# A hybrid decoder layer on one core: 24 instead of 16 tokens gathered, adds ahead of softmaxes, memory loads at other points

## The chip, the cores and the metric

The kernel runs on 1 core of one Trainium2 chip. The metric is the device time of one execution in microseconds (us).
## The reference

One inference step of a decoder layer, in float32, for 256 prompt tokens and 64 sample tokens (8 requests of 8 tokens) that share the weights:

```
x = x + merge(dilated_attention(h), window_attention(h))   # h = rmsnorm(x), one input projection
x = x + cross_attention(rmsnorm(x), memory keys, memory values)   # 4 heads of 128, 256 memory tokens
x = x + peer(rmsnorm(x))
y = rmsnorm(x)

def peer(xb):            # 128*128 experts of one neuron, 8 heads, the 16 best of each head
    q = (xb @ w_pq).reshape(T, 8, 256)
    s1, s2 = q[..., :128] @ sub_k1.T, q[..., 128:] @ sub_k2.T
    # top 16 of each half, top 16 of their 256 sums -> eidx (T, 8, 16), gate = softmax(best)
    act = gelu(einsum('td,thkd->thk', xb, expert_u[eidx]))
    return einsum('thk,thkd->td', gate * act, expert_v[eidx])
```

The model width is 2048; expert_u and expert_v have 16384 rows of 2048 float32 each, 128 MB apiece.

## The kernel before

The 320 tokens lie as two groups of columns: tile 0 (128 tokens, `FIRST_TILE`) and the rest (192 tokens, `THE_REST`: 128 of the prompt, called tile 1 below, and the 64 sample tokens). Up to about 460 us the input projection and the prompt attention run. From there to about 665 us a loop over the 8 requests (`for n in range(REQ)`, lines 1115 and 1715) does the sample attention; between its steps TensorE does output projection, cross-attention query and output tiles of tile 0 (`OUT_WITH`, line 98: which tiles stand ahead of the scores, with the scores, and with the turning of the probabilities). VectorE adds each output tile to the stream (`add_to_stream`, line 887) and does the softmax of the next request (`softmax_s`). A tile may start when the tile two before it has been added, as two PSUM banks take turns. Then, to about 1000 us, come the output projection, cross-attention and query projection of the rest, with tile 0's expert choice on VectorE between them.

SP loads all dense weights as chunks of 1 MB into a ring of four slots (`WR`); a chunk's load is issued when TensorE has used the chunk four before it. `mem_keys(g)` (2 MB) and `mem_values(g)` (four times 0.5 MB) load the memory of requests 4g to 4g+3 in that same list of SP, both g into the same buffers (`km`, `vm`).

The experts are done in two ways. For tile 0, each of the 128 (head, k) choices is one **row**: an indirect DMA by POOL brings one expert of each of the 128 tokens (1 MB, line 539 for expert_u, line 545 for expert_v), and VectorE does the dot product (`u_dot`, line 1240) or the weighted sum (`v_row`, line 1253). Sixteen tokens of tile 1 (`FEW`) are gathered too: their 8 heads stand on 8 groups of 16 partitions, so 16 more rows do for all of them. Rows in all: `ROWS` = 144 for u and 144 for v. Three buffers (`URING`) take the u rows, four (`VRING`) the v rows; a gather is issued when the row three (four) before it has been used. The other 176 tokens (`DENSE`) are multiplied with all experts: 128 chunks of expert_u, then 128 chunks of expert_v, each chunk 16 matmuls of 128x128 by 128x176. Every float32 matmul is two instructions on PE, so a chunk is 32. Their gates are built as maps: VectorE makes one-hots from the turned choices (line 1354), ScalarE weighs them (line 793), TensorE multiplies them (4 tokens, 8 instructions a map), VectorE applies them (line 1364). There are `MAPS` = 44 maps, spread over the u chunks from `MAP_LO` = 100 to 124.

The order around the change, by position: VectorE has done u rows 0 to 140 (`ROWS_BEFORE` = 141) and then copies the turned choices (lines 1343 to 1345) and signals `choices_kept`; TensorE turns the choices after u chunk 91 (`TURN` = 92) and waits for `choices_kept` at the first map, in chunk 100. ScalarE moves the choices of the 16 tokens to other partitions with 8 small DMAs after chunk 79 (`few_choices_in`); POOL waits for them ahead of row 128. From chunk 103 on (`DOTS_DONE` = 102) VectorE's slots between the maps, 1 or 2 rows a chunk, hold v rows. After v chunk 95 TensorE adds the sum of the 16 tokens (`h_few`) through `pick`.

## Time and profile before

| what | value |
|---|---|
| median of 3 runs | 2308.41 us (2307.99 to 2311.57) |
| the profiled execution's own time | 2311.11 us |
| its span in the trace | 2309.2 us |
| PE, PEld, DVE, ACT, POOL busy | 96%, 87%, 51%, 13%, 17% |
| granted PE clock over the span | 0.984 |
| moved by DMA | 843.21 MB, mean 365 GB/s |

Times inside the trace count from the start of the span. "Busy" of PE is modelled for pipelined matmuls, so a PE that is 100% busy may still start its matmuls at a slower pace; the number of instructions in a stretch tells the pace. What stands in square brackets behind a row of a timeline is the idle time ahead of it and what ended it.

### The profile page before, as it was taken

What the parts mean: (1) busy time and instruction counts of PE and PEld (TensorE: products, weight loads), DVE (VectorE), ACT (ScalarE), POOL (GpSimd) and SP (SyncE); (2) the same over time, 40 slices, a digit from 0 to 9 for tenths busy, and PEclk for the clock granted to TensorE, in tenths of its full rate; (3) what the DMA queues carried; (4) which work ended last, traced back from release to release, by engine and by line L of the source; (5) the groups of instructions that cost most, each with busy time, mean ns of one, the idle gap of its engine ahead of it and who ended that gap; (6) DMA issues with size and microseconds to landing.
All of it is one profiled execution on the core that took longest, in us unless ns stands there. A gap on an engine that the chain in (4) does not pass through costs nothing.

```text
span 2309.2 us, 35404 instructions
## 1 busy us (share of the span) xinstructions
PE 2207.9 (96%) x14282; PEld 2015.7 (87%) x14282; DVE 1179.1 (51%) x2095; ACT 301.2 (13%) x926; POOL 386.3 (17%) x414
## 2 busy tenths in 40 slices
PE   7999998789889879999999999999999999999998
PEld 5677776577589868999999999899999999999998
DVE  3200003833566647767777544599744444444422
ACT  2000001722221012011111110144200000000000
POOL 0100000022302011232212221133311111111100
PEclk9999999999999989999999999999999999999999
DMA  7999982289959898999999999999999999999974
GB/s 280 405 413 381 385 316 81 80 333 357 398 201 396 345 383 315 407 398 422 422 421 420 420 420 420 372 372 376 402 422 421 422 422 421 422 422 422 421 315 155
DMA packets 117787, 843.21 MB, mean 365 GB/s; under 512 B 14432, under 2 KB 16608, under 8 KB 30656
## 3 DMA queue, kind: packets, MB, share of 16 engines
q1 hardware_dynamic: 62752, 485.30, 52.4%
q0 software_dynamic: 54128, 354.58, 37.7%
q10 hardware_dynamic: 816, 2.11, 0.2%
q8 instruction: 58, 0.95, 0.2%
q14 instruction: 33, 0.27, 0.0%
HBM read 834.25 MB, written 74.78 MB: 394 GB/s over the span
## 4 chain that ended last, share of the span: by engine, by line
PE 64%; DMA 23%; DVE 8%; issue 2%; ACT 1%; POOL 1%; SPq 0%; DVEq 0%; POOLq 0%; ACTq 0%
PE low L1414 39%; PE big L1414 24%; DMA BIG<-expert_u,VB 20%; DVE BIG L1240 4%; DMA WR<-wall 1%; DMA BIG<-kaT 1%; ACT BIG L630 1%; DMA BIG<-expert_v,VB 1%; DMA BIG<-memT 0%; DMA BIG<-va 0%; DVE CST L968 0%; POOL BIG L525 0%; DVE BIG L846 0%; PE low L1538 0%; DVE HT L883 0%
## 5 line engine op out<-in xcount | busy, mean ns | idle before, releaser
L1414 PE MATMUL low<-HT,WR 128*128 128x176 f32 (+3 forms) x6336 | 1081.9, 333 | 8.4 <-DMA WR<-wall 7.0
L1414 PEld LDWEIGHTS low<-HT,WR 128*128 128x128 f32 x6336 | 984.2, 191 | 98.2 <-issue 9.7
L1414 PE MATMUL big<-BIG,WR 128*128 (+3 forms) x2888 | 450.7, 312 | 11.3 <-DVE XT L891 7.1
L1253 DVE SCALAR_TENSOR_TENSOR XT<-BIG,VB,XT 128x2048 f32<-128x2048 f32 x128 | 300.9, 2351 | 302.7 <-DMA BIG<-expert_v,VB 302.4
L1414 PE MATMUL low<-BIG,WR 128*128 (+3 forms) x2616 | 434.8, 321 | 12.6 <-DMA WR<-wall 10.3
L1414 PEld LDWEIGHTS big<-BIG,WR 128*128 128x128 f32 x2888 | 419.3, 193 | 30.1 <-issue 18.5
L1240 DVE SCALAR_TENSOR_TENSOR BIG<-BIG 128x2048 f32<-128x2048 f32 x144 | 329.5, 2291 | 210.8 <-DMA BIG<-expert_u,VB 209.7
L1414 PEld LDWEIGHTS low<-BIG,WR 128*128 128x128 f32 x2616 | 411.0, 192 | 17.8 <-issue 10.5
L539 POOL DMA_INDIRECT BIG<-expert_u,VB x144 | 161.5, 1122 | 683.8 <-DVE BIG L1240 609.5
L545 POOL DMA_INDIRECT BIG<-expert_v,VB x144 | 161.5, 1122 | 558.2 <-DVE XT L1253 477.3
L914 DVE TENSOR_SCALAR BIG<-low 128x320 f32 x32 | 15.7, 492 | 264.0 <-PE low L1414 264.0
L1414 PE MATMUL big<-BIG 128*32 128x256 f32 (+4 forms) x868 | 80.5, 376 | 16.1 <-issue 8.9
L1414 PEld LDWEIGHTS big<-BIG 128*32 128x32 f32 (+2 forms) x868 | 52.7, 141 | 36.5 <-issue 14.6
L777 ACT ACTIVATE BIG<-low 128x176 f32 x100 | 31.8, 318 | 334.3 <-PE low L1414 324.2
L819 ACT ACTIVATE HT<-XT 128x2048 f32<-128x2048 f32 x1 | 1.9, 1910 | 557.1 <-DVE XT L1253 557.1
L793 ACT ACTIVATE HT<-HT,VB 128x128 f32<-128x128 f32 x176 | 56.2, 390 | 89.9 <-DVE HT L1354 89.9
L1354 DVE TENSOR_TENSOR HT<-CST,VB 128x512 f32<-128x512 f32 x88 | 56.6, 684 | 7.7 <-PE big L1414 7.7
L1414 PE MATMUL big<-HT 128*128 128x128 f32 x352 | 47.9, 280 | 5.0 <-ACT HT L793 5.0
L1414 PEld LDWEIGHTS big<-HT 128*128 128x128 f32 x352 | 45.5, 194 | 5.6 <-issue 5.5
L511 POOL DMA_DIRECT2D HT<-kbT x1 | 0.5, 536 | 266.8 <-PE low L1414 266.8
L525 POOL DMA_DIRECT2D BIG<-kaT x56 | 29.8, 539 | 81.2 <-PE low L1414 81.2
L622 ACT ACTIVATE BIG<-low 128x512 f32<-128x512 f32 (+3 forms) x5 | 2.3, 466 | 293.3 <-PE low L1500 293.3
(230 smaller groups left out, 1124.0 us busy)
## 6 DMA issues: line engine op xcount, KB each, us to landing
WR<-uT SPq DMA_DIRECT2D x128, 1024.0 KB
WR<-expert_v SPq DMA_DIRECT2D x128, 1024.0 KB
WR<-wall SPq DMA_DIRECT2D x122, 1024.0 KB
BIG<-va POOLq DMA_DIRECT2D x48, 512.0 KB, 11.0
BIG<-kaT POOLq DMA_DIRECT2D x64, 384.0 KB, 11.0
BIG<-kmT SPq DMA_DIRECT2D x2, 2048.0 KB, 12.9
BIG<-vm SPq DMA_DIRECT2D x8, 512.0 KB, 13.4
XT<-xT SPq DMA_DIRECT2D x1, 2560.0 KB, 21.9
```

The costliest lines, as they stand in the source:

```text
L525: pool.dma_start(kr[j][:, NEWK:SW], d["kaT"][n, j, :, FIRST:PAST]).then_inc(s_kr[j], 16)
L539: nc.gpsimd.indirect_dma_start(u_ring[n % URING], None, d["expert_u"], bass.IndirectOffsetOnAxis(eidx[:, n:n + 1], 0)).then_inc(s_ug[n % U ...
L545: nc.gpsimd.indirect_dma_start(v_ring[n % VRING], None, d["expert_v"], bass.IndirectOffsetOnAxis(eidx[:, v_slot(n):v_slot(n) + 1], 0)).the ...
L622: nc.scalar.activation(VT[0:m, t, q * 512:q * 512 + w], bank[3 + n % 2][0:m, 0:w], ACT.Copy).then_inc(s_vtev, 1)
L630: ins = nc.scalar.activation(pb[:, s, lo:hi], pb[:, s, lo:hi], ACT.Exp, bias=stat[:, c:c + 1], scale=1.0, accum_out=stat[:, c + 4:c + 5])
L777: nc.scalar.activation(C[:, bass.ds(i * (UB * DENSE) + r * DENSE, DENSE)], u_out[r], ACT.Gelu).then_inc(s_dev, 1)
L793: nc.scalar.activation(x, x, ACT.Copy, scale=turned[2][:, 4 * g + j:4 * g + j + 1]).then_inc(s_weighed, 1)
L914: nc.vector.tensor_scalar(QK[:, bass.ds(i * (4 * NT) + r * NT, NT)], bank[r % 2][:, 0:NT], 1.0, None, ALU.mult).then_inc(s_ev, 1)
L1240: nc.vector.scalar_tensor_tensor(out=u, in0=u, scalar=1.0, in1=h_tok if n < SLOTS else h_few, op0=ALU.mult, op1=ALU.mult, accum_out=dots[: ...
L1253: nc.vector.scalar_tensor_tensor(out=x_tok, in0=rows_of(row), scalar=weight, in1=x_tok, op0=ALU.mult, op1=ALU.add).then_inc(s_vsum, 1)
L1354: ins = nc.vector.tensor_tensor(hot[z][g % 2], iota.unsqueeze(1).broadcast_to([P, 4, NKEY]), turned[z][:, 4 * g:4 * g + 4].unsqueeze(2).br ...
L1414: return nc.tensor.matmul(out, lhsT, rhs, start=start, stop=stop, skip_group_check=True)
```

## The change

It does five things.

- Eight more tokens of tile 1 are gathered (`FEWER`). Their (head, k) choices stand on 128 partitions as two halves of k, 8 heads and 8 tokens, so 8 more rows hold them: `ROWS` is 152, `DENSE` 168, `MAPS` 42. Per head there are two more small DMAs on ScalarE's queue (24 in all).
- The activations of the eight tokens are copied over `h_tok` after row 127, turned by TensorE and written back by ScalarE. These 16 transposes stand after the turning of the choices, at chunk 92, and wait for `choices_kept` and the copy.
- With 152 rows, `DOTS_DONE` becomes 108. `h_few` is used twice: 16 rows, then 40 rows of tile 0, then the 8 rows; TensorE adds the two sums after v chunks 31 and 95.
- In the loop over the requests VectorE does the adds of the tiles "with scores", the norm of request 3 and two query copies of request 4 ahead of the softmax instead of behind it. The last cross-attention output tiles of tile 0 use three banks.
- SP issues the first memory keys and values three chunks later; half of the second values get buffers of their own and are issued right behind them.

The changed lines:

```diff
-FEW = 16
+FEW, FEWER = 16, 8
+ALONE = FEW + FEWER
...
-DENSE = REST - FEW
+DENSE = REST - ALONE
...
-ROWS = SLOTS + FEW
+ROWS = SLOTS + FEW + FEWER
+ROOM = 22528
+V_FEW = (*range(SLOTS, SLOTS + FEW), *range(40), *range(SLOTS + FEW, ROWS), *range(40, SLOTS))
+FEWER_AT = V_FEW.index(SLOTS + FEW)
...
-FEW_OUT = 96
+FEW_OUT, FEWER_OUT = 32, 96
...
-        vm = [BIG[:, at:at + 1024] for at in (4096, 13440, 22528, 23552)]
+        vm = [[BIG[:, at:at + 1024] for at in ats] for ats in ((4096, 13440, 22528, 23552), (6656, 14784, 4096, 13440))]
...
-        few_src = HT[0:FEW, :].rearrange("p (k t) -> p k t", t=NT)[:, 14:16, 0:P]
+        few_src, fewer_src = (HT[a:b, :].rearrange("p (k t) -> p k t", t=NT)[:, 14:16, 0:P] for a, b in ((0, FEW), (FEW, ALONE)))
...
+        pick_fewer = VB[:, 3 * ROWS + 3 * DENSE + FEW:3 * ROWS + 3 * DENSE + ALONE]
...
-                at = f % 2 if stage == "pq" else 5 + f % 2
+                at = f % 2 if stage == "pq" else (5, 6, 0)[(f - 6) % 3] if stage == "co" and f >= 6 else 5 + f % 2
...
+        s_fewout = sem("few_added")
...
-            return SLOTS + n if n < FEW else n - FEW
+            return V_FEW[n]
...
-            def mem_values(g):
-                for n in range(4):
-                    sp.dma_start(vm[n], d["vm"][4 * g + n]).then_inc(s_vm[g], 16)
+            def mem_values(g, lo, hi):
+                for n in range(lo, hi):
+                    sp.dma_start(vm[g][n], d["vm"][4 * g + n]).then_inc(s_vm[g], 16)
...
-                if before == POS["out", 1, 15]:
+                if before == POS["cq", 1, 0]:
...
-                    mem_values(0)
+                    mem_values(0, 0, 4)
+                    sp.wait_ge(s_sc, 3)
+                    sp.wait_ge(s_idx, 3)
+                    mem_values(1, 0, 2)
...
-                    mem_values(1)
+                    mem_values(1, 2, 4)
...
-                    pool.wait_ge(s_few, 16 * PH)
+                    pool.wait_ge(s_few, 16 * 3 * PH)
...
-                act.dma_start(chosen[FEW * h:FEW * (h + 1), :, SLOTS:ROWS], few_src[:, :, h * PK:(h + 1) * PK]).then_inc(s_few, 16)
-            dense_gelu(TAIL, MAP_LO)
+                act.dma_start(chosen[FEW * h:FEW * (h + 1), :, SLOTS:SLOTS + FEW], few_src[:, :, h * PK:(h + 1) * PK]).then_inc(s_few, 16)
+                for half in range(2):
+                    to, k = half * 64 + h * FEWER, h * PK + half * FEWER
+                    act.dma_start(chosen[to:to + FEWER, :, SLOTS + FEW:ROWS], fewer_src[:, :, k:k + FEWER]).then_inc(s_few, 16)
+            dense_gelu(TAIL, TURN)
+            keep_rows(4, h_tok, big)
+            dense_gelu(TURN, MAP_LO)
...
-                if n + 1 < REQ:
-                    softmax_s(n + 1)
-                for f in (*with_scores, *with_turn):
+                for f in with_scores:
...
-                if n < 3:
-                    for f in range(max(5 * n - 1, 0), 5 * n + 4):
-                        group_square(FIRST_TILE, CROSS, f)
...
-                    for f in range(1, 4):
-                        keep_cross_query(FIRST_TILE, f)
+                    keep_cross_query(FIRST_TILE, 1)
+                    keep_cross_query(FIRST_TILE, 2)
+                if n + 1 < REQ:
+                    softmax_s(n + 1)
+                for f in with_turn:
+                    add_to_stream(FIRST_TILE, CROSS, f)
+                if n < 3:
+                    for f in range(max(5 * n - 1, 0), 5 * n + 4):
+                        group_square(FIRST_TILE, CROSS, f)
+                if n == 4:
+                    keep_cross_query(FIRST_TILE, 3)
...
+                if n == SLOTS + FEW:
+                    dve.wait_ge(s_ht, 4)
...
-                nc.vector.scalar_tensor_tensor(out=u, in0=u, scalar=1.0, in1=h_tok if n < SLOTS else h_few, op0=ALU.mult, op1=ALU.mult, accum_out=dots[:, n:n + 1]).then_inc(s_udot, 1)
+                nc.vector.scalar_tensor_tensor(out=u, in0=u, scalar=1.0, in1=h_few if SLOTS <= n < SLOTS + FEW else h_tok, op0=ALU.mult, op1=ALU.mult, accum_out=dots[:, n:n + 1]).then_inc(s_udot, 1)
...
-                if n == 0:
+                slot = v_slot(n)
+                if slot == SLOTS + FEW:
+                    dve.wait_ge(s_fewout, 1)
+                if slot in (SLOTS, SLOTS + FEW):
...
-                elif n < FEW:
+                elif slot > SLOTS:
...
+                    link(nc.vector.tensor_reduce(pick_fewer, ident.rearrange("p (h t) -> p t h", t=FEWER), AX_X, ALU.add))
...
-                        first = slice(0, FEW)
+                        first = slice(0, ALONE)
...
+                if n == SLOTS - 1:
+                    dve.wait_ge(s_udot, SLOTS)
+                    nc.vector.tensor_copy(h_tok.rearrange("p (k h t) -> p k h t", k=KT, h=P // FEWER), HT_by[:, :, P + FEW:P + ALONE].unsqueeze(2).broadcast_to([P, KT, P // FEWER, FEWER])).then_inc(s_rep, 1)
...
-            dve.wait_ge(s_few, 16 * PH)
-            own = P - FEW
+            dve.wait_ge(s_few, 16 * 3 * PH)
+            own = P - ALONE
...
-                nc.vector.tensor_copy(turned[z][:, 0:own], bank[6][:, z * P + FEW:(z + 1) * P])
+                nc.vector.tensor_copy(turned[z][:, 0:own], bank[6][:, z * P + ALONE:(z + 1) * P])
...
-                    pe.wait_ge(s_xadd[g], KT + f - 1 - g)
+                    pe.wait_ge(s_xadd[g], KT + f - (1 if g == FIRST_TILE and f < 8 else 2))
+                if g == FIRST_TILE and f == 8:
+                    pe.wait_ge(s_smax, 2 * REQ)
...
-                            ins = mm(bank[5][32 * n:32 * n + 32, :], pT[:, b * P + 32 * n:b * P + 32 * n + 32], vm[n][:, b * 512:(b + 1) * 512], start=(b == 0), stop=(b == 1))
+                            ins = mm(bank[5][32 * n:32 * n + 32, :], pT[:, b * P + 32 * n:b * P + 32 * n + 32], vm[r][n][:, b * 512:(b + 1) * 512], start=(b == 0), stop=(b == 1))
...
-                return mm(u_out[r], WR[:, slot_of(r) * D + k * P:slot_of(r) * D + (k + 1) * P], HT[:, k * NT + P + FEW:(k + 1) * NT], start=(k == 0), stop=(k == KT - 1))
+                return mm(u_out[r], WR[:, slot_of(r) * D + k * P:slot_of(r) * D + (k + 1) * P], HT[:, k * NT + P + ALONE:(k + 1) * NT], start=(k == 0), stop=(k == KT - 1))
...
+            pe.wait_ge(s_turnev, 1)
+            pe.wait_ge(s_rep, 2)
+            turn_rows(h_tok, P)
...
-                    pe.wait_ge(s_turnev, 1)
+                    pe.wait_ge(s_ht, 4)
...
-                    ins = mm(v_all[k][:, FEW:REST], WR[:, slot_of(r) * D + k * P:slot_of(r) * D + (k + 1) * P], coefs, start=(first and k % 2 == 0), stop=last)
+                    ins = mm(v_all[k][:, ALONE:REST], WR[:, slot_of(r) * D + k * P:slot_of(r) * D + (k + 1) * P], coefs, start=(first and k % 2 == 0), stop=last)
...
-                mm(v_all[k][:, 0:FEW], h_few[:, k * P:(k + 1) * P], pick, start=False, stop=True)
-            v_chunks(FEW_OUT, MAP_LO)
+                ins = mm(v_all[k][:, 0:FEW], h_few[:, k * P:(k + 1) * P], pick, start=False, stop=True)
+            ins.then_inc(s_fewout, 1)
+            v_chunks(FEW_OUT, FEWER_OUT)
+            pe.wait_ge(s_vsum, FEWER_AT + FEWER)
+            for k in range(KT):
+                mm(v_all[k][:, FEW:ALONE], h_few[:, k * P:(k + 1) * P], pick_fewer, start=False, stop=True)
+            v_chunks(FEWER_OUT, MAP_LO)
```

On TensorE, at the end of the u chunks up to 91, there stands before:

```order
L1871 MATMUL big<-CST,HT 128x128 [waits gates_ready,k_scores_kept]
L1871 MATMUL big<-CST,HT 128x128 x2
L1414 MATMUL big<-CST,HT 64x64 x6
L1859 UNCONDITIONAL_BRANCH
L1859 ISA
L1862 ISA [waits chunk_in0]
L1414 MATMUL low<-HT,WR 128x176 [waits dense_gelu]
```

and in the changed kernel (the lines moved down by some 27):

```order
L1900 MATMUL big<-CST,HT 128x128 [waits gates_ready,k_scores_kept]
L1900 MATMUL big<-CST,HT 128x128 x2
L1441 MATMUL big<-CST,HT 64x64 x6
L1795 MATMUL big<-CST,BIG 128x128 [waits few_repeated,choices_kept]
L1795 MATMUL big<-CST,BIG 128x128 x15
L1888 UNCONDITIONAL_BRANCH
L1888 ISA
L1891 ISA [waits chunk_in0]
L1441 MATMUL low<-HT,WR 128x168 [waits dense_gelu]
```

The 16 transposes and their wait for `choices_kept` now stand ahead of chunks 92 to 99; the wait used to stand in chunk 100.

On SP, in the list of weight loads (`wall`) around the memory loads, there stands before:

```order
L484 DMA WR<-wall 128x2048 [waits chunk_used] x47
L460 DMA BIG<-kmT 128x4x1024 [waits chunk_used]
L464 DMA BIG<-vm 128x1024 x4
L484 DMA WR<-wall 128x2048 [waits chunk_used] x7
L460 DMA BIG<-kmT 128x4x1024 [waits c_scores]
L484 DMA WR<-wall 128x2048 [waits chunk_used] x2
L464 DMA BIG<-vm 128x1024 [waits c_request_values]
L464 DMA BIG<-vm 128x1024 x3
```

and in the changed kernel:

```order
L493 DMA WR<-wall 128x2048 [waits chunk_used] x50
L466 DMA BIG<-kmT 128x4x1024 [waits chunk_used]
L470 DMA BIG<-vm 128x1024 x4
L470 DMA BIG<-vm 128x1024 [waits experts_chosen,k_scores]
L470 DMA BIG<-vm 128x1024
L493 DMA WR<-wall 128x2048 [waits chunk_used] x4
L466 DMA BIG<-kmT 128x4x1024 [waits c_scores]
L493 DMA WR<-wall 128x2048 [waits chunk_used] x2
L470 DMA BIG<-vm 128x1024 [waits c_request_values]
L470 DMA BIG<-vm 128x1024
```

Three chunk loads moved from behind the first memory loads to ahead of them, and two of the four second value loads moved up.

On VectorE, at the softmax of request 2, there stands before:

```order
L1063 COPY BIG<-big 64x8x8 x3
L1024 SCALAR_TENSOR_TENSOR BIG<-low,HT 128x64 [waits s_turned,s_scores,keys_used]
L1025 SCALAR_TENSOR_TENSOR BIG<-low,HT 128x256
...
L1034 TENSOR_SCALAR CST<-CST 128x1 [waits dve_chain]
L891 TENSOR_TENSOR XT<-XT,big 128x128 [waits chunk_used] x4
```

and in the changed kernel:

```order
L1077 COPY BIG<-big 64x8x8 x3
L905 TENSOR_TENSOR XT<-XT,big 128x128 [waits chunk_used] x2
L1038 SCALAR_TENSOR_TENSOR BIG<-low,HT 128x64 [waits s_turned,s_scores,keys_used]
L1039 SCALAR_TENSOR_TENSOR BIG<-low,HT 128x256
...
L1048 TENSOR_SCALAR CST<-CST 128x1 [waits dve_chain]
L905 TENSOR_TENSOR XT<-XT,big 128x128 [waits chunk_used] x2
```

Two of the four adds moved from behind the softmax to ahead of it.

## Rows read from the trace of the kernel before

**Rows 1.** Windows: stretch, length, busy time (instructions) of each engine, clock, DMA share, GB/s.

```profile
1100.00:1150.00 50.00, 50.00 (x338) 50.00 (x337) 37.94 (x82) 5.76 (x13) 10.94 (x10) 1.00 1.01 422
1550.00:1600.00 50.00, 50.00 (x364) 49.94 (x363) 49.59 (x63) 22.68 (x91) 17.76 (x11) 1.00 0.98 383
```

**Rows 2.** DMA queues, 1700 to 2100 us: packets, MB, share of the 16 engines.

```profile
q1 hardware_dynamic: 11587, 84.34, 50.7%
q0 software_dynamic: 11583, 84.37, 50.7%
```

**Rows 3.** Timeline, PE: one tile each of 192 and of 176 columns.

```profile
891.63 2.76 PE L1414 MATMUL low<-BIG,WR 128*128 128x192 f32 x16
...
1658.79 2.55 PE L1414 MATMUL big<-BIG,WR 128*128 128x176 f32 x16
```

**Rows 4.** Timeline, ACT: eight small DMAs, GELU of chunks 83 and 84.

```profile
1379.26 5.26 ACTq L786 DMA_DIRECT2D VB<-HT x8
...
1398.20 0.32 ACT L777 ACTIVATE BIG<-low 128x176 f32 x1 [4.46 <-PE low L1414]
1403.30 0.32 ACT L777 ACTIVATE BIG<-low 128x176 f32 x1 [4.78 <-PE low L1414]
```

**Rows 5.** Timeline, PE: chunks 92 to 100, and the first map.

```profile
1438.81 41.74 PE L1414 MATMUL low<-HT,WR 128*128 128x176 f32 x274
1485.50 2.05 PE L1414 MATMUL big<-HT 128*128 128x128 f32 x8 [4.95 <-ACT HT L793]
```

**Rows 6.** Timeline, DVE: row 140, the first copy of the choices, the first one-hots.

```profile
1479.44 2.29 DVE L1240 SCALAR_TENSOR_TENSOR BIG<-BIG 128x2048 f32<-128x2048 f32 x1 [2.67 <-DMA BIG<-expert_u,VB]
...
1481.65 0.27 DVE L1343 COPY VB<-big 128x112 f32<-128x112 f32 x1
...
1483.63 2.50 DVE L1354 TENSOR_TENSOR HT<-CST,VB 128x512 f32<-128x512 f32 x4
```

**Rows 7.** Timeline, DVE: a u row while TensorE takes no chunks.

```profile
1006.49 2.29 DVE L1240 SCALAR_TENSOR_TENSOR BIG<-BIG 128x2048 f32<-128x2048 f32 x1 [0.46 <-DMA BIG<-expert_u,VB]
```

**Rows 8.** Lines: the 16 transposes of h_few.

```profile
L1766 PE MATMUL big<-CST,BIG x16: 272/272/273, 916.2 to 917.9; 128*128 128x128 f32 x16
```

**Rows 9.** Timeline, PE: two maps in a row of the middle stretch.

```profile
1603.36 1.05 PE L1414 MATMUL big<-HT 128*128 128x128 f32 x8
...
1606.94 1.05 PE L1414 MATMUL big<-HT 128*128 128x128 f32 x8
```

**Rows 10.** Timeline, DVE: v rows 32 and 143 (the last).

```profile
1665.22 2.35 DVE L1253 SCALAR_TENSOR_TENSOR XT<-BIG,VB,XT 128x2048 f32<-128x2048 f32 x1 [2.37 <-DMA BIG<-expert_v,VB]
...
2219.47 2.35 DVE L1253 SCALAR_TENSOR_TENSOR XT<-BIG,VB,XT 128x2048 f32<-128x2048 f32 x1 [2.63 <-DMA BIG<-expert_v,VB]
```

**Rows 11.** Timeline, the end: tile 0's square, the squares of the rest, the last sum.

```profile
2221.86 1.91 ACT L819 ACTIVATE HT<-XT 128x2048 f32<-128x2048 f32 x1 [557.08 <-DVE XT L1253]
...
2289.59 4.80 ACT L825 ACTIVATE BIG<-XT 128x192 f32<-128x192 f32 x16 [65.41 <-DVE XT L1397]
...
2293.18 5.36 PE L1414 MATMUL big<-BIG,CST 128*128 128x192 f32 x32
```

**Rows 12.** Timeline, PE: first and last of three waits, loop over requests.

```profile
520.69 8.99 PE L1414 MATMUL big<-BIG,WR 128*128 128x128 f32 x64 [3.53 <-DVE XT L891]
...
600.78 3.84 PE L1414 MATMUL big<-BIG,WR 128*128 128x128 f32 x32 [3.54 <-DVE HT L1073]
```

**Rows 13.** Windows in that loop (columns as in rows 1).

```profile
550.00:560.00 10.00, 7.61 (x43) 7.61 (x44) 2.71 (x9) 0.51 (x2) 0.00 (x0) 0.66 0.77 307
610.00:620.00 10.00, 9.31 (x105) 5.16 (x99) 6.93 (x27) 4.73 (x16) 5.72 (x11) 1.00 1.02 405
```

**Rows 14.** Timeline, cross-attention of the rest: two waits of PE, one row of DVE.

```profile
808.65 6.52 PE L1414 MATMUL low<-HT,WR 128*128 128x192 f32 x22 [6.99 <-DMA WR<-wall]
...
865.12 3.64 PE L1414 MATMUL big<-BIG 128*32 128x512 f32 x16 [8.89 <-issue]
...
871.30 2.29 DVE L1240 SCALAR_TENSOR_TENSOR BIG<-BIG 128x2048 f32<-128x2048 f32 x1 [3.06 <-DMA BIG<-expert_u,VB]
```

More of the change, by code:

```diff
@@ L167, in build @@
         HT = region("HT", KT * NT)
-        BIG = region("BIG", NCH * DENSE + (URING + 2) * D)
+        BIG = region("BIG", ROOM + (URING + 2) * D)
         OT = BIG[:, 0:KT * NT]
@@ L257, in build @@
         C_by = C.rearrange("p (c t) -> p c t", t=DENSE)
-        h_few = BIG[:, NCH * DENSE:NCH * DENSE + D]
-        u_ring = [BIG[:, NCH * DENSE + (1 + r) * D:NCH * DENSE + (2 + r) * D] for r in range(URING)]
-        h_tok = BIG[:, NCH * DENSE + (URING + 1) * D:NCH * DENSE + (URING + 2) * D]
+        h_few = BIG[:, ROOM:ROOM + D]
+        u_ring = [BIG[:, ROOM + (1 + r) * D:ROOM + (2 + r) * D] for r in range(URING)]
+        h_tok = BIG[:, ROOM + (URING + 1) * D:ROOM + (URING + 2) * D]
         v_ring = u_ring + [h_tok]
```

## The prediction

> **What bounds the kernel now.** I read the forty slices and the windows first, then the queues, then the timelines of PE and DVE where a wait is moved. PE is busy 96%, but that is an average over stages with different limits. From 1050 to 1480 us (u chunks) and 1650 to 2220 us (v chunks) the DMA engines are full: 422 GB/s, share 1.01 [rows 1]. There POOL's queue and SP's carry the same, 84.37 and 84.34 MB in 400 us [rows 2], one row (1.0486 MB) for each chunk: 2 x 1.0486 MB / 422 GB/s = 4.97 us a pair. A chunk costs PE 4.77 us at 176 columns. By the tiles of 192 and 176 columns, (2.76 - 2.55) / 16 = 0.013 us an instruction for 16 columns [rows 3], so 168 columns cost 4.77 - 32 x 0.0066 = 4.56 us. The gap between two GELUs is 5.10 us in these stretches [rows 4], above 4.77: arrival sets the pace and PE waits a little in each chunk. A chunk with fewer columns gains nothing there. In the map stretch (1485.5 to 1658.8 us) DMA is below full (383 GB/s) and both PE (364 instructions in 50 us) and DVE (49.59 of 50) are busy [rows 1].
>
> **The turn's wait.** Before, PE works through chunks 92 to 99 (from 1438.81 us) while DVE is still at its u rows [rows 5]. Row 140 starts at 1479.44, the copies of the choices at 1481.65, and the first one-hots at 1483.63, so the copies take 2.0 us; the first map stands at 1485.50 [rows 5, 6]. The change keeps "u rows 0 to 140, then the copies", but puts the wait for `choices_kept` at chunk 92. PE then stops at about 1439 until the copies are done, and eight chunks come behind the wait that used to cover it. While PE stands, the ring of four chunks fills, about 1439 + 3 x 4.97 = 1454 us; from then POOL has all DMA to itself. A row in such a time followed the last within 2.29 + 0.46 = 2.75 us [rows 7] instead of 4.97. From 1454 to 1479 five rows were due; they take 14 us instead of 25, so row 140 is about 10 us earlier than otherwise. Bounds: 0.46 us is DVE's least wait and 3 us its common one in the unsaturated time, so 8 us at least; 15 to 20 if the early gain below gives its DMA time to the rows too. With T for the end of row 140's dot product, the first map stood at T + 3.8 us before. After the change come the copies 2.0, 16 transposes (as those of `h_few`, from 916.2 to 917.9, about 1.8 [rows 8]), a clock restart of 3 (behind a wait of 6.99 us, 22 instructions took 6.52 us where they need 3.3 at full clock [rows 14]), eight chunks of 4.56 = 36.5 from a full ring, and the part of chunk 100 ahead of the map, 2.85. That is T + 46. So 42 us later, less the 10 by which T is earlier: **+33** (28 to 36). Named again: TensorE stands for some 1481 - 10 + 2 - 1439 = 34 us.
>
> The small DMAs: eight took 5.26 us on ACT, 0.66 each [rows 4]; 24 take 15.8. The next GELU is late by that, and PE may run two `low` banks ahead. The bound is 0 to 11 us for PE; I take 0 net, because the wait 8 chunks later is for a row, not for PE: what PE loses here, it would have waited.
>
> **The map stretch.** Two maps fewer, and 8 columns fewer in some 33 chunks. PE's work falls by 2 x 1.05 + 33 x 0.2 = 8.7 us, DVE's by two maps. Two maps in a row of PE start 3.58 us apart [rows 9], while DVE is full [rows 1] and keeps its 36 v rows of work between them. DVE's part of a map is 3.58 us less a share of a row, at least 1.9. Two of them: 3.8 to 7.2. I take **-5** (-3 to -8).
>
> **The v stretch and the tail.** The v rows in the map stretch start at chunk 109 instead of 103 and are 25 instead of 33 when v chunk 0 starts. Before, rows 32 to 143 lie between 1665.22 and 2219.47: 111 x 4.993 us [rows 10]. After, 127 are left: 127 x 4.97 = 631, plus the one under way, 638. The chunks, 128 of them at 4.97, ran 634 us before (1658.79 to 2293.18 [rows 3, 11]) and cannot become shorter by columns while rows run beside them; before, the last 70 us had no rows and PE's 4.77 set the pace there. Now rows and chunks end together. Chunks end at +635 if each has a row beside it. What was hidden far ahead of the end now lies near it: tile 0's square at 2221.86 had 65 us before the squares of the rest [rows 11]. Its 1.91 us, and at most the 4.80 us of the 16 squares, come behind the last row, with the write of tile 0. **+6.5** (2 to 9).
>
> **The request loop.** Three times PE waits 3.5 us for an add or a copy that stood behind a softmax (3.53, 3.53, 3.54; first and last shown [rows 12]). With the adds ahead, these 10.6 us go. DMA had a dip there, 307 GB/s beside 405 60 us later [rows 13]: PE's next tiles are wall chunks, and where DMA is at 405 they come no sooner. I take **-7** (-4 to -10.6). The softmax of the next request is two adds later, 2 x 0.3 us, with PE's output tiles as cover.
>
> **Cross-attention of the rest.** PE waits 6.99 us for a weight chunk queued behind 4 MB of memory keys and values, and 8.89 us for the second values [rows 14]; the clock is at its lower level behind each. Three chunks now stand ahead of the first memory loads, and 1 MB of the second values goes with them (both semaphores it waits for are past by then; SP's chunk loads stand behind these). Both waits, about 15.9 us, may go, and 2 us of clock. But the bytes are the same, and DVE, too, waited there for a gathered row (3.06 us at 871.30, ahead of what PE's output tiles need [rows 14]). Half: **-10** (-5 to -18). The third bank for tile 0's last output tiles is at 0: the adds behind them set that pace.
>
> The sum is +33 - 5 + 6.5 - 7 - 10 = **+17.5 us**. On the profiled execution's 2311.11 us that is 2328.6; the median of the runs is 2.7 lower, so 2325.9 us.
>
> **Two pages weighed.** The Trainium skill, "DMA: Bandwidth & Descriptors", section "Where 436 GB/s comes from", puts the binding limit of HBM to SBUF for one core at about 358 GB/s. The trace shows 422 [rows 1]. By the page's figure a pair would take 5.86 us instead of 4.97, and no part of the sum could be so; the measurement decides (the same section lists 425 GB/s for one measurement, which agrees). The section "Queues, rings and completion order" of the same page says that the DMA engines go round between queues. By that rule a faster PE gets no more than its half of the DMA, and the rows none of its spare half until SP's ring is full; the equal 84 MB agree [rows 2].
>
> **The rivals.**
> *Level.* As above, but all early gains come (-10.6 - 17 = -27.6) and row 140 is 15 us earlier, since DMA had room from 750 to 925 us: +28 for the turn, -5, +3. Sum about -2: 2307 to 2312.
> *Faster, the other side.* While TensorE stands, the rows have all DMA, and what PE lost is given back because fewer bytes compete: row 140 then comes 20 us earlier (eight chunk loads of 2.49 us not ahead of it), +42 - 20 = +22; with -27.6 early, -8 in the map stretch and +2 at the end, -11: 2297. It decides where row 140 is at least 16 us early, and all 15.9 us of the memory waits go. For it: rows at 2.75 us are possible [rows 7]. Against it: at 1439 SP's four slots are still to be filled, and they get half.
> *Much slower.* The memory loads behind three more chunks come too late: PE waits for them as before, and only the request loop gains (-7, 0, +36, -3, +9 = +35): 2343. It decides if keys or values land later than PE reaches them; against it, 1 MB less is left for the last.
> *The change does not do what it says.* Only if `choices_kept` came with an earlier row; DVE's list still has 141 rows ahead of it, so 1% and no more.
>
> **How the numbers follow.** Chances: the forecast 0.64, level 0.15, faster 0.14, much slower 0.07. A measurement of this kernel can tell about 0.2%, 4.6 us. The forecast's own range is the sum of the bounds, not all at once: 2314 to 2336. The range of 8 in 10 takes in most of the level case: 2304 to 2337. Faster by over 0.2%: the faster case and a little of level, 0.16. Within: most of level, 0.13. Slower: 0.71.
>
> **What the profile after would show.** PE idle for 25 to 38 us behind chunk 91, ended by DVE (the copies behind row 140), with u rows 2.8 us apart in that time and a lower clock just behind; the first map 39 us after the last transpose; chunks of 4.6 us for some four chunks after the restart. Three waits of 3.5 us gone from the request loop; the first u chunk's GELU some 17 us earlier. V rows until within 10 us of the last v chunk; v chunks 4.97 us apart to the end. Wrong would be: row 140 at 1455 or earlier (then level or faster), no idle time at the turn, or a memory wait of over 5 us that stays.

## The result, and the profile after

The changed kernel takes 2337.3 us (median of 4 runs, 2334.0 to 2339.8), the kernel before 2308.2 us (4 runs, 2305.2 to 2311.6). The ratio is 1.0117, with a 95% interval of 1.0101 to 1.0133: slower by some 27 us by the ratio and 29 us by the medians, where 17.5 us slower was forecast. The median lies 0.3 us above the stated range of 2304 to 2337 us.

The page of the changed kernel: busy time of each engine, then the granted clock, the DMA share and GB/s in 40 slices of 58 us. The last line is the GB/s of the kernel before.

```profile
PE 2178.4 (93%) x14314; PEld 1966.5 (84%) x14314; DVE 1213.4 (52%) x2115; ACT 297.8 (13%) x917; POOL 399.9 (17%) x430
...
PEclk9999999999999989999999997999999999999998
DMA  7999962299969889999999998689999999999996
GB/s 305 391 414 398 392 254 80 91 365 411 359 235 404 335 359 365 409 411 421 422 421 422 421 419 342 224 345 407 400 422 422 422 422 422 422 422 421 421 422 274
...
GB/s 280 405 413 381 385 316 81 80 333 357 398 201 396 345 383 315 407 398 422 422 421 420 420 420 420 372 372 376 402 422 421 422 422 421 422 422 422 421 315 155
```

PE has 30 us less work and is idle for longer. In slices 25 to 27 (1403 to 1578 us) DMA is at 342, 224 and 345 GB/s, where it was at 420, 372 and 372 before. The waits of PE, summed by line and releaser, name the place (total, times, longest):

```profile
PE big L1795 <- DVE VB L1372: 42.2, 1, 42.2
```

The timeline of PE around the turn, which answers [rows 5]:

```profile
1424.07 0.73 PE L1441 MATMUL big<-CST,HT 64*64 64x64 f32 x12
1466.99 3.67 PE L1795 MATMUL big<-CST,BIG 128*128 128x128 f32 x16 [42.19 <-DVE VB L1372]
1470.45 40.24 PE L1441 MATMUL low<-HT,WR 128*128 128x168 f32 x276
1510.53 1.05 PE L1441 MATMUL big<-HT 128*128 128x128 f32 x8
```

PE stands for 42.2 us behind chunk 91, until VectorE has done row 140 and the copies. Then come the transposes, chunks 92 to 99, and the first map at 1510.5 us, where it was at 1485.5.

VectorE in that time, which answers [rows 6, 7]: rows 127, 128 and 140, and the first copy.

```profile
1404.41 2.29 DVE L1260 SCALAR_TENSOR_TENSOR BIG<-BIG 128x2048 f32<-128x2048 f32 x1 [2.82 <-DMA BIG<-expert_u,VB]
...
1417.38 2.29 DVE L1260 SCALAR_TENSOR_TENSOR BIG<-BIG 128x2048 f32<-128x2048 f32 x1 [9.41 <-DMA BIG<-expert_u,VB]
...
1462.78 2.31 DVE L1260 SCALAR_TENSOR_TENSOR BIG<-BIG 128x2048 f32<-128x2048 f32 x1 [0.79 <-DMA BIG<-expert_u,VB]
...
1465.02 0.26 DVE L1370 COPY VB<-big 128x104 f32<-128x104 f32 x1
```

Row 128 starts 13.0 us behind row 127, not 5. POOL's timeline shows why:

```profile
1392.41 0.94 POOL L548 DMA_INDIRECT BIG<-expert_u,VB  x1 [4.07 <-DVE BIG L1260]
1407.76 1.02 POOL L548 DMA_INDIRECT BIG<-expert_u,VB  x1 [14.41 <-DMA VB<-HT]
```

POOL may not gather row 128 until the 24 small DMAs have landed. ScalarE issued them from 1365.5 to 1383.0 us, and by the end of POOL's wait the last landed at about 1407.7. Eight of them, before, made no such wait.

Windows over the stop and behind it (columns as in [rows 1]):

```profile
1444.00:1467.00 23.00, 0.01 (x1) 0.01 (x1) 15.61 (x22) 0.00 (x0) 8.59 (x8) 0.50 0.90 333
1467.00:1510.00 43.00, 43.00 (x289) 43.00 (x290) 2.46 (x4) 6.09 (x16) 0.00 (x0) 0.94 0.57 204
```

The stop costs DMA time twice. While TensorE stands, the rows alone draw 333 GB/s, not 422. While it then works off the chunks, VectorE has only one-hots, no row is asked for (POOL is at 0.00), and DMA runs at 204.

The end, which answers [rows 11]: ScalarE's square of tile 0 and its squares of the rest, VectorE's last three rows and first adds, the last sum on PE.

```profile
2316.46 1.91 ACT L833 ACTIVATE HT<-XT 128x2048 f32<-128x2048 f32 x1 [632.58 <-DVE XT L1276]
...
2318.70 4.14 ACT L839 ACTIVATE BIG<-XT 128x192 f32<-128x192 f32 x16
...
2309.13 7.30 DVE L1276 SCALAR_TENSOR_TENSOR XT<-BIG,VB,XT 128x2048 f32<-128x2048 f32 x3 [2.59 <-DMA BIG<-expert_v,VB]
2316.34 2.20 DVE L1424 TENSOR_TENSOR XT<-XT,big 128x192 f32<-128x192 f32 x8
...
2319.19 8.44 PE L1441 MATMUL big<-BIG,CST 128*128 128x192 f32 x32 [5.02 <-DVE XT L1424]
```

The v rows now end behind the last chunk. PE waits 5.0 us, and the last sum takes 8.44 us instead of 5.36; the mean granted clock from 2319 to 2328 us is 0.65, between the chip's two levels. The wait is put down to VectorE's adds, but the first of them was done before 2316.7 us. PE's last sum reads ScalarE's squares of the rest, and ScalarE does tile 0's square ahead of these: its first square of the rest starts 2.4 us behind the first add, and 0.4 us behind it before (2289.59 and 2289.20 us). So some 2 us of the 5.0 are tile 0's square.

The way from before to after, in milestones of the two profiled executions (us):

| milestone | before | after | later by |
|---|---|---|---|
| end of the request loop (norm sum of tile 0) | 663.9 | 656.2 | -7.7 |
| last scores kept, ahead of u chunk 0's GELU | 992.7 | 982.4 | -10.3 |
| turn (behind chunk 91) | 1438.2 | 1424.1 | -14.1 |
| first map | 1485.5 | 1510.5 | +25.0 |
| v chunk 0 | 1658.8 | 1677.5 | +18.7 |
| last sum starts | 2293.2 | 2319.2 | +26.0 |
| end of span | 2309.2 | 2338.0 | +28.8 |

### The profile page after: what moved, and what is told of

It reads as the page before. It is cut to its first block, busy times and chain, and to the rows that moved or that the text cites. A ratio compares the mean times of both kernels' runs of the same rounds, so it can differ in the third digit from the quotient of the medians.

```text
span 2338.0 us, 35528 instructions
## 1 busy us (share of the span) xinstructions
PE 2178.4 (93%) x14314; PEld 1966.5 (84%) x14314; DVE 1213.4 (52%) x2115; ACT 297.8 (13%) x917; POOL 399.9 (17%) x430
## 3 DMA queue, kind: packets, MB, share of 16 engines
q0 software_dynamic: 56432, 371.35, 39.1%
## 4 chain that ended last, share of the span: by engine, by line
DMA 49%; PE 32%; DVE 12%; issue 4%; ACT 1%; POOL 1%; SPq 0%; DVEq 0%; POOLq 0%; ACTq 0%
DMA BIG<-expert_v,VB 25%; PE low L1441 23%; DMA BIG<-expert_u,VB 19%; PE big L1441 8%; DVE BIG L1260 4%; DVE XT L1276 3%; DMA BIG<-kaT 2%; DMA WR<-wall 2%; DMA BIG<-va 1%; ACT BIG L639 1%; DVE HT L1381 1%; DVE BIG L1274 1%; DMA BIG<-memT 0%; POOL BIG L534 0%; POOL BIG L548 0%
## 5 line engine op out<-in xcount | busy, mean ns | idle before, releaser
L1441 PE MATMUL low<-HT,WR 128*128 128x168 f32 (+3 forms) x6360 | 1064.0, 328 | 15.2 <-DMA WR<-wall 6.8
L1441 PEld LDWEIGHTS low<-HT,WR 128*128 128x128 f32 x6360 | 959.4, 191 | 112.7 <-issue 21.1
L1260 DVE SCALAR_TENSOR_TENSOR BIG<-BIG 128x2048 f32<-128x2048 f32 x152 | 347.8, 2291 | 203.5 <-DMA BIG<-expert_u,VB 202.1
L1441 PE MATMUL big<-BIG,WR 128*128 (+3 forms) x2888 | 435.3, 306 | 15.6 <-DMA WR<-expert_v 5.7
L1441 PEld LDWEIGHTS big<-BIG,WR 128*128 128x128 f32 x2888 | 403.8, 192 | 40.8 <-issue 39.2
L1441 PE MATMUL low<-BIG,WR 128*128 (+3 forms) x2616 | 421.2, 316 | 17.3 <-DMA WR<-wall 10.6
L1441 PEld LDWEIGHTS low<-BIG,WR 128*128 128x128 f32 x2616 | 398.8, 192 | 22.2 <-issue 10.7
L548 POOL DMA_INDIRECT BIG<-expert_u,VB x152 | 177.4, 1167 | 743.8 <-DVE BIG L1260 653.8
L928 DVE TENSOR_SCALAR BIG<-low 128x320 f32 x32 | 15.7, 492 | 264.0 <-PE low L1441 264.0
L786 ACT ACTIVATE BIG<-low 128x168 f32 x100 | 30.9, 311 | 327.8 <-PE low L1441 292.1
L1274 DVE SCALAR_TENSOR_TENSOR BIG<-BIG,VB 128x2048 f32<-128x2048 f32 x22 | 51.7, 2349 | 20.7 <-DMA BIG<-expert_v,VB 20.3
L1795 PE MATMUL big<-CST,BIG 128*128 128x128 f32 x32 | 5.6, 349 | 42.2 <-DVE VB L1372 42.2
```

What stands on the lines that cost most here:

```text
L548: nc.gpsimd.indirect_dma_start(u_ring[n % URING], None, d["expert_u"], bass.IndirectOffsetOnAxis(eidx[:, n:n + 1], 0)).then_inc(s_ug[n % U ...
L786: nc.scalar.activation(C[:, bass.ds(i * (UB * DENSE) + r * DENSE, DENSE)], u_out[r], ACT.Gelu).then_inc(s_dev, 1)
L928: nc.vector.tensor_scalar(QK[:, bass.ds(i * (4 * NT) + r * NT, NT)], bank[r % 2][:, 0:NT], 1.0, None, ALU.mult).then_inc(s_ev, 1)
L1260: nc.vector.scalar_tensor_tensor(out=u, in0=u, scalar=1.0, in1=h_few if SLOTS <= n < SLOTS + FEW else h_tok, op0=ALU.mult, op1=ALU.mult, a ...
L1274: nc.vector.scalar_tensor_tensor(out=h_few, in0=row, scalar=weight, in1=h_few, op0=ALU.mult, op1=ALU.add).then_inc(s_vsum, 1)
L1441: return nc.tensor.matmul(out, lhsT, rhs, start=start, stop=stop, skip_group_check=True)
```

## The experiments

Eleven kernels ran, in three groups. Each is given with its ratio to the kernel before, measured beside it on the same chip (the medians of before were 2310.4, 2308.9 and 2312.3 us in the three groups). "Turn to map" is the time from the turn's last matmuls to the first map in the profile: 47.4 us before, 86.5 us after. One profile tells a place in time to some 4 us only: with the same code up to there, the turn stands at 1438.2 and 1440.4 us in two kernels, and at 1424.1 and 1419.9 in two others.

### The wait alone

To the kernel before, one line is added:

```diff
             ins.then_inc(s_turn, 1)
+            pe.wait_ge(s_turnev, 1)
```

> The kernel before with one wait more: TensorE waits for the copies of the choices ahead of chunk 92. No further tokens, no transposes, nothing else changed. Theory A (the place of this wait is the cost of the change): TensorE stands 34 to 37 us behind chunk 91, the first map comes about 32 us later than 1485.5 us, and the whole is 27 to 32 us slower than before, 2336 to 2341. Rival (the further tokens, their rows and transposes are the cost): under 15 us slower, 2323 or less.

Measured: 2342.7 us, ratio 1.014 (1.0113 to 1.0167), 30 us slower by the medians. Its timeline of PE:

```profile
1440.43 0.73 PE L1414 MATMUL big<-CST,HT 64*64 64x64 f32 x12
1476.09 43.07 PE L1414 MATMUL low<-HT,WR 128*128 128x176 f32 x274 [34.93 <-DVE VB L1345]
1519.00 1.05 PE L1414 MATMUL big<-HT 128*128 128x128 f32 x8
```

Without a further token or transpose, the wait alone gives a loss as large as that of the changed kernel: a stop of 34.9 us, turn to map 78.6 us instead of 47.4, so +31.2. Theory A holds.

### The copies ahead of row 130

In the changed kernel the nine copies and their signal move in VectorE's list, and nothing else:

```diff
             while row[0] < ROWS_BEFORE:
                 n = row[0]
+                if n == 130:
+                    dve.wait_ge(s_turn, 1)
+                    dve.wait_ge(s_few, 16 * 3 * PH)
...
+                    ins.then_inc(s_turnev, 1)
+                    dve.wait_ge(s_turnev, 1)
```

> The changed kernel with VectorE's copies of the turned choices ahead of row 130 of expert_u instead of behind row 140; rows 130 to 140 still stand ahead of the first one-hots. Theory A: TensorE's stop at chunk 92 shrinks from 42 us to under 8, chunks 92 to 99 run beside the rows again, the first map comes at about 1483 us instead of 1510.5, and all of that stays: about 2310. Rival B (while TensorE stood, the rows had the DMA to themselves, so most of the stop is given back): row 140 comes later by what the rows now share, and the whole gains 10 us or less, 2327 or more.

Measured: 2306.6 us, ratio 0.9978 (0.9965 to 0.999); against the changed kernel that is 31 us less. PE's two waits there:

```profile
1426.81 1.97 PE L1795 MATMUL big<-CST,BIG 128*128 128x128 f32 x16 [2.01 <-DVE VB L1358]
...
1478.35 2.05 PE L1441 MATMUL big<-HT 128*128 128x128 f32 x8 [10.24 <-ACT HT L807]
```

The stop is down to 2.0 us, turn to map to 54.3 us. Rival B, by which the rows give most of the stop back, falls. With the run above, the cause is shown from both sides: put into the old kernel it costs 30 us, taken out of the new one it gives 31.

### The early edits alone, and one of them

The first kernel has VectorE's new order in the request loop, the memory loads at their new places and the third bank, on the kernel before. The second has the loop's order only (its core):

```diff
-                if n + 1 < REQ:
-                    softmax_s(n + 1)
-                for f in (*with_scores, *with_turn):
+                for f in with_scores:
...
+                if n + 1 < REQ:
+                    softmax_s(n + 1)
+                for f in with_turn:
```

> The kernel before with the early edits alone: adds ahead of softmaxes, memory loads at other points, third bank for tile 0's last output tiles; no further tokens gathered. Theory A (rows set the first map): TensorE comes to chunk 0 of expert_u about 10 us earlier, as in the changed kernel, but row 140 of expert_u comes only 2 to 3 us earlier, because the DMA is full; so the wait at the first map grows from 5 to about 13 us and the whole gains 2 to 4 us: 2304 to 2306. Rival B (TensorE sets it): all 10 us stay, 2298.

> The kernel before with the VectorE order of the request loop alone (adds with the scores ahead of the softmax). Both theories: the three waits of 3.5 us are gone and the loop ends 7 to 8 us earlier. Theory A: at most 3 us of it is left at the first map and at the end, 2305 to 2307. Rival B: all of it stays, 2300 to 2301.

Measured: 2299.3 us for all early edits, ratio 0.994 (0.992 to 0.9961); 2304.2 us for the loop, ratio 0.9973 (0.9962 to 0.9984). My theory A had come after the result, from row 140 being earlier by less than PE was. It fell for both by the profiles: in the loop's kernel the turn is 7.7 us earlier and the first map 8.3 us. The time of that kernel, though, lies between the two theories (2305 to 2307 and 2300 to 2301). In the early-edits kernel the turn is 12.3 us earlier and row 140 starts at 1467.0 instead of 1479.4, 12.4 us earlier; the wait at the first map is unchanged:

```profile
1473.08 2.05 PE L1421 MATMUL big<-HT 128*128 128x128 f32 x8 [4.96 <-ACT HT L796]
```

So rows do not hold back an early gain. They start earlier too (row 0 at 691.3 instead of 699.6 us), and then go one for one with the chunks. By the medians the loop's order is worth 6 us and the other early edits 5 us more (2 us more in the spans of the two profiled executions).

### The changed kernel without the early edits

> The changed kernel without the early edits: old VectorE order in the loop, old places of the memory loads, two banks. 24 tokens are gathered as in the changed kernel. Theory A: the stop at the turn shrinks from 42 us to 33 to 35 us, since TensorE comes 10 us later and row 140 only 2 to 3 us later; the whole is 2 to 4 us slower than the changed kernel, 2339 to 2341. Rival B: the early gain of 10 us is missing in full, 2347.

Measured: 2344.4 us, ratio 1.0142 (1.0125 to 1.0159), 7 us slower than the changed kernel by the medians and 6 by the ratios, whose intervals overlap. The stop is 41.5 us, so it did not shrink. Theory A fell here too; rival B's sign and rough size hold, with 7 us in place of 10. Its turn is at 1432.7 us, 8.6 us behind that of the changed kernel, and its first map 7.9 us.

### The small DMAs earlier

```diff
-EXPS, TAIL = 64, 80
+EXPS, TAIL = 64, 72
```

> The changed kernel with the 24 small DMAs of ScalarE after chunk 71 instead of 79. In the changed kernel POOL waits 14.4 us for them ahead of row 128 of expert_u, which starts 13.0 us behind row 127 instead of 5. Theory C (this delay is a part of the stop at the turn): the gap falls to 5 us, the stop from 42 to about 34 to 37 us, and the whole gains 5 to 8 us, 2329 to 2332. Rival D (the rows make the 8 us up while TensorE stands): within 1 us of the changed kernel, 2337.

Measured: 2333.1 us, ratio 1.0106 (1.009 to 1.0123), 4 us less than the changed kernel by the medians and 2.5 by the ratios; the intervals overlap, so the profile says more than the time. The gap from row 127 to 128 is 5.0 us, the stop 38.8 us:

```profile
1463.84 3.68 PE L1795 MATMUL big<-CST,BIG 128*128 128x128 f32 x16 [38.81 <-DVE VB L1372]
```

Of the 8 us by which row 128 was late, 3.4 reach the stop; the rest had been made up at the faster pace of rows while TensorE stood. The truth is between C and D: POOL's wait was a part of the stop, and less than half of it counted.

### Both repairs together

> The changed kernel with the copies ahead of row 130 and the 24 small DMAs after chunk 71. Theory C: row 140 comes 7 to 8 us earlier than with the early copies alone, the wait at the first map falls from 10.2 to about 4 us, and the whole gains 5 to 8 us on that: 2299 to 2302, level with the kernel before that has the early edits alone. Rival D: no gain, 2306 to 2307.

Measured: 2306.4 us, ratio 0.9989 (0.9977 to 1.0002), level with the copies at row 130 alone. C fell; rival D has the time right. VectorE's timeline shows the reason:

```profile
1424.58 0.27 DVE L1356 COPY VB<-big 128x104 f32<-128x104 f32 x1 [5.91 <-PE big L1441]
...
1426.53 2.29 DVE L1260 SCALAR_TENSOR_TENSOR BIG<-BIG 128x2048 f32<-128x2048 f32 x1
```

With its rows on time, VectorE reaches the copies 5.9 us before TensorE has turned the choices, and waits. What the small DMAs gave is lost in a wait the other way.

### Fewer rows ahead of the maps

On the kernel with the early edits alone:

```diff
-ROWS_BEFORE = 141
+ROWS_BEFORE = 138
```

> The kernel before with the early edits, and 138 rows of expert_u instead of 141 ahead of the copies and the first maps. If the 4.96 us wait at the first map is a loss of its own, it goes and the whole gains 3 to 5 us on the early edits alone: 2295. If the map stretch is bound by VectorE, which now has three more u rows in it and the same v rows to come, the gain is 0 to 2 us: 2298.

Measured: 2298.6 us, ratio 0.9955 (0.9937 to 0.9973), the same as with 141 rows. The first map comes 4.9 us earlier, at 1468.2 us, but v chunk 0 only 2.5 us (1645.2 instead of 1647.6): the map stretch grew from 174.6 to 177.0 us, and PE waits 3.8 us in it later. The wait at the first map was no loss of its own that the times would show.

And on the changed kernel, with the copies ahead of row 132 and the small DMAs after chunk 71, 138 and 135 rows ahead of the maps:

> The changed kernel with the copies ahead of row 132, the small DMAs after chunk 71 and 138 rows ahead of the first maps. With the copies at row 130 and the small DMAs early, VectorE came to the copies before TensorE had turned the choices, waited some 5 us, and the first map waited 9.5 us for rows. Theory: copies two rows later cost TensorE 3 to 5 us at chunk 92, both waits behind it go, the first map is at 1473 to 1475 us, and the whole is 2 to 4 us faster than with row 130: 2302 to 2304. Rival: the rows that are missing ahead of the maps come back one for one in the map stretch, 2306.

> The same with 135 rows ahead of the first maps. If the map stretch is bound by VectorE, the three further rows in it cost what they save ahead of it, and the result is that of 138 rows within 2 us; if rows ahead of the maps are still what the first map waits for, it is 3 to 5 us faster, under 2300.

Measured: 2309.2 us (0.9993, 0.9981 to 1.0005) and 2318.7 us (1.0029, 1.0014 to 1.0044). Both expectations failed: with 138 rows 2302 to 2304 was expected (the rival: 2306), with 135 the same as with 138 or faster. The waits at the first map are gone (it stands at 1470.6 and 1468.9 us, where 1473 to 1475 was expected for 138 rows), and v chunk 0 is early too (1642.6 and 1641.4), but at the end PE waits, with 138 rows and then with 135:

```profile
2289.28 7.05 PE L1441 MATMUL big<-BIG,CST 128*128 128x192 f32 x32 [8.19 <-DVE XT L1424]
```

```profile
2298.19 7.89 PE L1441 MATMUL big<-BIG,CST 128*128 128x192 f32 x32 [20.70 <-DVE XT L1424]
```

With 152 rows it is the rows that end last. A u row put into the map stretch pushes a v row out of it, and three such rows more (135 instead of 138) make the last sum start 8.9 us later, at 2298.2 instead of 2289.3 us: 3.0 us for a row behind the last chunk. The medians differ by 9.4 us. The expectation for 135 rows looked at the maps only.

### Sixteen v rows less

In the changed kernel the last 16 rows of expert_v of tile 0 are neither gathered nor summed, so tile 0's output lacks them. VectorE's line of the edit (POOL's loop and ScalarE's wait are shorter by the same 16):

```diff
-            for n in range(n_v, ROWS):
+            for n in range(n_v, ROWS - 16):
```

> The changed kernel without the last 16 rows of expert_v of tile 0: they are neither gathered nor summed, so tile 0's output lacks them. Theory E (rows and chunks each take half of the DMA, and only the tail waits for the rows): chunks beside rows stay 4.97 us apart, the last 16 or so come at 4.6, and the wait of 5.0 us and the slower last sum are gone; the whole gains 11 to 14 us, 2324. Rival F (the v stretch costs its bytes): 16 x 2.49 = 40 us less, 2297.

Measured: 2322.1 us, ratio 1.0063 (1.0045 to 1.008): 15 us less than the changed kernel by the medians, 12 by the ratios. Theory E holds. The last sum has no wait and its old length:

```profile
2303.01 5.36 PE L1441 MATMUL big<-BIG,CST 128*128 128x192 f32 x32
```

From v chunk 0 to it are 631.6 us instead of 641.7, and 3.1 us more are saved in it. Together that is 13 us. Sixteen rows are 16 x 2.49 = 40 us of DMA time, but the chunks beside the other rows do not use it: the v stretch does not cost its bytes.

## Why the prediction was right or wrong

**The turn's wait: right in kind and place, +33 forecast, 39.1 measured** (from -14.1 at the turn to +25.0 at the first map), outside its bounds of 28 to 36. In the kernel with the wait alone the step's figures are confirmed: the stop 34.9 us where 34 was worked out, turn to map +31.2, and row 140 starts 31.2 us behind the turn instead of 41.3, so 10.1 us earlier where 10 was forecast. Two things in that were off and cancelled. Rows while TensorE stands follow 3.1 to 3.4 us apart, not 2.75 (from row 135 to 140 15.7 us in the kernel with the wait alone, from row 132 to 140 26.8 us in the changed one); in the latter POOL waits 2.2 to 3.6 us for VectorE's release ahead of five of its gathers. But SP's ring was full 10 us behind the stop and not 15, so the rows had the DMA sooner.

In the changed kernel the other half of the step holds too: from the end of row 140 (1465.0) to the first map it takes 45.5 us, and 46 was forecast. The term that was mis-sized is the 10 us by which row 140 was to come earlier: it starts 38.7 us behind the turn, only 2.6 us earlier. Of the 7.5 us that are missing, 3.4 are the small DMAs, the next point. The rest is a lead of TensorE over the rows that the prediction did not have. Row 127 starts 23.3 us ahead of the turn in the kernel before and with the wait alone, 19.7 us in the changed kernel and 19.4 with the small DMAs earlier; over all profiles it is 23.3 to 24.6 us with chunks of 176 columns and 17.4 to 22.5 with 168. TensorE comes to the turn sooner than the rows do, and stands for that much longer.

**The small DMAs: wrong.** The prediction set them at 0 by looking at who waits for ScalarE. ScalarE's GELUs were late (three in a row at 1383 us), and PE had cover, as said. The step that failed is that it named no cost for the landing: POOL's row 128 waits for the last of 24, and they landed 25 us behind the last issue, where DMA was full. Earlier, they give 3.4 us at the stop, and 2.5 to 4 us in the whole. The Trainium skill, "DMA: Bandwidth & Descriptors", section "Queues, rings and completion order", says that each DMA engine goes round the queues packet by packet. The late landing of few bytes beside two full queues does not contradict it, but no run here changes the load beside them alone, so the reason for the 25 us is not shown.

**The request loop: right.** -7 forecast, 7.7 us at the loop's end, 6 us in the whole with that edit alone. The reason given for taking less than 10.6 holds as well: the three waits are gone, and PE waits for loads instead. Before, then after:

```profile
PE low L1414 <- DMA BIG<-kaT: 2.8, 5, 1.8
PE big L1414 <- DMA BIG<-va: 1.0, 2, 0.8
...
PE low L1441 <- DMA BIG<-kaT: 6.2, 12, 1.8
PE big L1441 <- DMA BIG<-va: 3.2, 5, 0.6
```

**Cross-attention of the rest: the size was wrong.** -10 forecast, 2.6 us measured in the changed kernel (from -7.7 to -10.3). The prediction read both waits as bytes in a full queue. In the changed kernel DMA is indeed full in both (424 GB/s from 812 to 820 us, 429 from 848 to 851), and "half" was then too much; no run moves these loads alone. In the changed kernel these waits of PE stand for [rows 14]:

```profile
819.91 5.49 PE L1441 MATMUL low<-HT,WR 128*128 128x128 f32 x32 [6.82 <-DMA WR<-wall]
...
850.79 3.56 PE L1441 MATMUL big<-BIG 128*32 128x512 f32 x16 [2.84 <-issue]
...
863.59 4.92 PE L1441 MATMUL low<-BIG,WR 128*128 128x192 f32 x16 [5.85 <-DVE BIG L1121]
```

The first wait moved by a few tiles and kept its length (6.99 to 6.82). That is one of the prediction's own signs of being wrong, a memory wait of over 5 us that stays. The second fell from 8.89 to 2.84, but the copy on VectorE behind a gathered row, which had cost 2.09 us, now costs 5.85.

**Fewer columns in the u chunks: small, and not nothing.** The prediction gave them 0 where the DMA is full. From the last scores to the turn the changed kernel takes 441.7 us instead of 445.5. Over all profiles it is 443.8 to 446.6 us in the five kernels with 176 columns (mean 445.1) and 441.1 to 445.0 in the eight with 168 (mean 442.7), so some 2 us are the columns'. In the changed kernel they are lost again, as TensorE then stands for longer.

**The map stretch: right.** -5 forecast, -6.4 measured (166.9 us instead of 173.3). What the prediction calls 36 v rows are 34 rows by the profiles: 3 u rows and 31 v rows before, 11 and 23 after.

**V stretch and tail: direction right, +6.5 forecast, +10.1 measured** (from +18.7 to +28.8). Of it 2.3 us are the stretch, 5.0 PE's wait, and 3.1 the last sum at a lower clock, which the prediction did not have. Of the v rows 129 were left at v chunk 0, not 127, but the last ended 639 us behind it, where 638 was worked out: the last three follow each other within 2.5 us. The prediction's term for tile 0's square (1.91 us) is in the 5.0, some 2 us of it; the rest of that wait is the last row, which ends 2.2 us behind PE's last chunk, and the first add and square.

**The sum.** -14.1 + 39.1 - 6.4 + 10.1 = 28.7 us against -17 + 33 - 5 + 6.5 = 17.5. The early gains were 3 us too high, the turn 6 us too low, the tail 4 us too low: no step had the wrong sign, and three (landing of small DMAs, TensorE's lead over the rows, clock behind a wait at the end) were left out. The measured sum lies nearer to the "much slower" rival (+35, chance 0.07) than to the forecast. Of the faster rival's two conditions one came true only in the letter: row 140 was 16.7 us earlier than before, but 14 of these came with PE itself. The other failed: of the 15.9 us of memory waits 9.7 stayed. The "much slower" rival fell on the second of these waits, but on the cross-attention (0, measured -2.6), on the turn (+36, measured 39.1) and on the tail (+9, measured 10.1) it was nearer than the forecast.

**What the change is worth without the wait.** The early edits alone give 2299 us, 11 us less than before by the medians and 14 by the ratio; with the 24 tokens and the copies moved, 2306.6. So gathering eight more tokens costs some 7 us even where the stop is down to 2.0 us. The two profiles put that loss behind the maps: v chunk 0 starts at 1647.6 and 1648.2 us, but the last sum at 2284.4 and 2288.8, and it takes 5.36 and 7.12 us. The rows then end last, while the narrower chunks have nothing to gain beside them. The best version measured is the early edits on 16 gathered tokens, ratio 0.994 (0.992 to 0.9961), with 138 or 141 rows ahead of the maps.

## What to carry to other kernels

A wait that is moved ahead of independent work loses the cover of that work, and its old length says nothing about its price: here 4.95 us became a stop of 34.9 us and a loss of 30 by the wait alone. So move its releaser too, and look for the wait the other way that this makes. Where two queues share a full DMA one to one, columns taken from the chunks in exchange for more rows paid nothing here once the rows ended last. For each small DMA, name who waits for its landing, not only who issues it.

## What the runs showed of the hardware

Twenty-four small DMAs of ScalarE, issued within 17.5 us beside two full queues, had the last one land 25 us after its issue (from 1383.0 us to the end of POOL's wait at 1407.8).

Gathers that were alone on the DMA, with three buffers, drew 333 GB/s (1444 to 1467 us) and not the 422 of two queues; the rows came 3.1 to 3.4 us apart.

Behind a wait of 5.0 us of PE, 32 matmul instructions of 192 columns took 8.44 us at a mean granted clock of 0.65, and 5.36 us where PE had worked until then. In the other kernels the same sum took 5.44 us behind a wait of 1.46 us, and 7.05 to 8.45 us behind waits of 3.8 to 20.7 us, with no order by the wait's length.
